# Expert stage 1 with 32 slots per expert in four 32-column tiles and 16 KB weight runs

## The reference

```python
D_MODEL = 1024; SEQ = 256; N_EXPERTS = 32; TOP_K = 2; EXPERT_FF = 512

def hier_moe(h, router_group_w, router_expert_w, w_gate, w_up, w_down):
    group_idx = argmax(h @ router_group_w)                 # 1 of 4 groups
    ...                                                    # top 2 of its 8 experts
    for each token n, each of its two experts e:
        a = h[n] @ w_gate[e]                               # 1024 -> 512
        b = h[n] @ w_up[e]
        out[n] += gate[n, e] * ((silu(a) * b) @ w_down[e]) # 512 -> 1024
```

## Time and profile before

| what | value |
|---|---|
| median of 3 runs | 2531.36 us (2530.78 to 2533.36) |
| span of the profiled execution | 2530.7 us |
| TensorE busy | 2299.3 us, 91% |
| VectorE busy | 1427.9 us, 56% |
| ScalarE busy | 1156.0 us, 46% |
| bytes moved | 653.96 MB, mean 258 GB/s |
| stage 1 in the span | about 258 to 779 us |

### The profile page before, as it was taken

The page is one execution under the profiler, slowest core; times in us unless marked ns, Lnnn a source line. Parts: engine busy times, 40 slices in busy tenths (PEclk is TensorE's granted clock), DMA queues, the critical chain, the costliest instruction groups (busy, mean ns, idle before and its releaser), DMA issues.

```text
span 2530.7 us, 31448 instructions
## 1 busy us (share of the span) xinstructions
PE 2299.3 (91%) x12724; PEld 1833.1 (72%) x12724; DVE 1427.9 (56%) x1373; ACT 1156.0 (46%) x999; POOL 289.0 (11%) x118
## 2 busy tenths in 40 slices
PE   6888899999997978998976789999999999999998
PEld 6877544444445977998875678787878787878786
DVE  4653211111113823453765178788888888888887
ACT  3521111111114523343543167676766766666765
POOL 4610000000002810002763000000000000000000
PEclk8998999999998999999988899999999999999999
DMA  7231699999995412555322159898989898989992
GB/s 258 91 128 67 238 394 394 394 394 394 394 394 183 138 51 84 185 183 183 134 100 100 67 199 366 306 365 308 368 305 370 302 370 308 365 312 361 335 335 112
DMA packets 286465, 653.96 MB, mean 258 GB/s; under 512 B 5312, under 2 KB 27968, under 8 KB 286144
## 3 DMA queue, kind: packets, MB, share of 16 engines
q1 hardware_dynamic: 286400, 653.01, 70.9%
HBM read 651.94 MB, written 1.05 MB: 258 GB/s over the span
## 4 chain that ended last, share of the span: by engine, by line
PE 78%; ACT 6%; DVE 6%; DMA 5%; issue 3%; POOL 1%; SPq 1%; ACTq 0%; POOLq 0%; DVEq 0%
PE psum L452 17%; PE psum L454 16%; PE psum L453 16%; PE psum L1395 7%; DMA ring<-in_w_up 5%; PE psum L582 3%; PE psum L1440 3%; PE psum L1380 2%; PE psum L1909 2%; PE psum L1422 2%; ACT arena_r L1737 1%; PE psum L1602 1%; DVE hT L435 1%; PE psum L425 1%; SPq L291 1%
## 5 line engine op out<-in xcount | busy, mean ns | idle before, releaser
L1796 DVE TENSOR_TENSOR ring_r<-ring,arena_r 128x2048 fp32r<-128x2048 f32 x338 | 766.6, 2288 | 175.8 <-ACT arena_r L1737 175.1
L1737 ACT ACTIVATE arena_r<-ring 128x2048 fp32r<-128x2048 f32 x338 | 633.3, 1911 | 221.6 <-PE psum L454 221.6
L453 PE MATMUL psum<-ring_r,arena_r 128*128 128x512 f32 (+1 forms) x1696 | 627.8, 370 | 0.0
L452 PE MATMUL psum<-arena_r 128*128 128x512 f32 (+1 forms) x1520 | 583.4, 384 | 15.2 <-DVE xT L1839 6.9
L454 PE MATMUL psum<-arena_r 128*128 128x512 f32 x1344 | 532.9, 397 | 0.0
L453 PEld LDWEIGHTS psum<-ring_r,arena_r 128*128 128x128 f32 x1696 | 320.8, 189 | 59.4
L452 PEld LDWEIGHTS psum<-arena_r 128*128 128x128 f32 x1520 | 286.2, 188 | 73.2 <-issue 11.8
L501 POOL TENSOR_TENSOR ring_r<-ring,ring_r 128x1024 fp32r<-128x1024 f32 x88 | 224.3, 2566 | 999.7 <-ACT ring_r L491 984.4
L454 PE MATMUL psum<-ring_r 128*128 128x256 f32 x1056 | 303.4, 287 | 0.0
L454 PEld LDWEIGHTS psum<-arena_r 128*128 128x128 f32 x1344 | 252.1, 188 | 59.2
L1395 PE MATMUL psum<-ring,arena 128*64 128x512 f32 x1024 | 224.5, 593 | 2.8 <-DMA ring<-in_w_up 1.8
(11 more groups left out here) (340 smaller groups left out, 2535.3 us busy)
## 6 DMA issues: line engine op xcount, KB each, us to landing
ring<-in_moe_w_gate SPq DMA_DIRECT2D x57, 2048.0 KB, 7.8
ring<-in_moe_w_up SPq DMA_DIRECT2D x56, 2048.0 KB, 7.8
ring<-in_moe_w_down SPq DMA_DIRECT2D x56, 2048.0 KB, 7.9
ring<-in_w_gate SPq DMA_DIRECT2D x32, 2048.0 KB, 15.7
ring<-in_w_down SPq DMA_DIRECT2D x32, 2048.0 KB, 12.6
ring<-in_w_up SPq DMA_DIRECT2D x32, 2048.0 KB, 19.3
ring<-in_c_w_in SPq DMA_DIRECT2D x8, 2048.0 KB, 9.1
ring<-in_w_in SPq DMA_DIRECT2D x7, 2048.0 KB, 17.5
```

The costliest lines, as they stand in the source:

```text
L452: nc.tensor.matmul(out, ah, bh, start=start, stop=False, **kw)
L453: nc.tensor.matmul(out, ah, bl, start=False, stop=False, **kw)
L1737: nc.scalar.activation(hi_buffer(j)[1], ring[:, m_ % SLOTS, half * HALF:(half + 1) * HALF], ACT.Copy).then_inc(weights_hi, 1)
L1796: nc.vector.tensor_tensor(ring_r[m_ % SLOTS][:, at], ring[:, m_ % SLOTS, at], hi_buffer(j)[1].bitcast(F32), ALU.subtract).then_inc(weights ...
```

## The change

C1 becomes 32, so two experts have 64 slots together (`PC`). Gate and up of both experts are now one group of matmuls: for each chunk k four tiles of 32 columns, gate 0, gate 1, up 0, up 1, which write partitions 0, 32, 64 and 96 onwards of bank 0. The down products also take four tiles, two experts by two halves of the result, in bank 2. Gathered tokens fit one bank and are copied in one step; the result is copied in two (L1530, L1531 of the changed file), from partitions 0 to 63 and 64 to 127. `gate_done` is gone: SP sends the gate and the up pieces when `up_done` arrives.

The rows of a weight piece are dealt as "(p k)": partition p gets eight (or four) neighbouring rows, one run of 16 KB. So that the products stay the same, the tokens' numbers are put in the matching order when they are transposed in the routing step, and the hidden values when silu is taken.

A trip starts with `share_transposed` and `spread_back` of the trip before, then gate/up, gather, down. The routing step writes its tables for eight rounds instead of four, with fewer and larger VectorE instructions.

```diff
-        C1, C2 = 64, 128
+        C1, C2 = 32, 128
         PASSES1, PASSES2 = T // C1, T // C2
...
-                return w[bass.ds(expert, 1), :, :].rearrange("e (k p) n -> p (e k) n", p=P), k, n
+                return w[bass.ds(expert, 1), :, :].rearrange("e (p k) n -> p (e k) n", p=P), k, n
...
-                    sp.wait_ge(moe_sems["moe1"][("gate_done", "up_done", "down_done")[s // 2]], i + 1)
+                    sp.wait_ge(moe_sems["moe1"]["up_done" if s < 4 else "down_done"], i + 1)
                     send(moe1_piece(expert[s % 2], s), s, landed["moe1"][s])
...
-                    sp.wait_ge(moe_sems["moe1"][("gate_done", "up_done", "down_done")[slot // 2]], trips1 + 1)
+                    sp.wait_ge(moe_sems["moe1"]["up_done" if slot < 4 else "down_done"], trips1 + 1)
...
-                    nc.scalar.activation(r_hrow[:, t * D + half * 512:t * D + half * 512 + 512], bank(2 * t + half),
-                                         ACT.Copy).then_inc(*s.step())
+                    row = r_hrow[:, t * D:(t + 1) * D]
+                    if m.groups:
+                        nc.scalar.activation(row.rearrange("p (k b c) -> p k b c", k=KC, b=KC)[:, :, 4 * half:4 * half + 4, :],
+                                             bank(2 * t + half).rearrange("p (b c k) -> p k b c", b=4, k=KC),
+                                             ACT.Copy).then_inc(*s.step())
+                    else:
+                        nc.scalar.activation(row[:, half * 512:half * 512 + 512], bank(2 * t + half),
+                                             ACT.Copy).then_inc(*s.step())
...
-            for p in range(m.passes):
-                do(nc.vector.tensor_copy(m.gate[:, :, m.per + p * n:m.per + (p + 1) * n], gt))
+            every = [P, NT, m.passes, n]
+            do(nc.vector.tensor_copy(m.by_pass(m.gate), gt.unsqueeze(2).to_broadcast(every)))
...
-            for p in range(1, m.passes):
-                do(nc.vector.tensor_scalar(w[:, 535 + p:536 + p], w[:, 534:535], float(p * m.slots), None, ALU.is_gt))
-            do(nc.vector.reduce_sum(w[:, 540:541], w[:, 536:535 + m.passes], AX_X))
+            over = w[:, 560:560 + m.passes - 1]
+            do(nc.vector.scalar_tensor_tensor(over, numbers[:, 1:], float(m.slots),
+                                              w[:, 534:535].to_broadcast([P, m.passes - 1]), ALU.mult, ALU.is_lt))
+            do(nc.vector.reduce_sum(w[:, 540:541], over, AX_X))
...
+        PC = 2 * C1
+        q_Xg, q_hidT = x_Xg[:, 0:KC * PC], x_hidT[:, 0:4 * PC]
+        q_silu, q_hid, q_y, q_shareT = (a[0:PC, :] for a in (x_silu, x_hid, x_y, x_shareT))
+
+        def pick_block(a, t, x, stride=PC):
+
+            return a[:, t * stride + x * C1:t * stride + (x + 1) * C1]
...
-                for r in range(2):
-                    for k in range(4 * r, 4 * r + 4):
-                        for t in range(NT):
-                            mm = nc.tensor.matmul(bank(7 - r)[:, (k % 4) * P:(k % 4 + 1) * P],
-                                                  r_hrow[:, t * D + k * P:t * D + (k + 1) * P],
-                                                  x_pick[:, t * P:(t + 1) * P], start=(t == 0), stop=(t == NT - 1))
-                    mm.then_inc(sem_["gathered"], 1)
+                pe.wait_ge(sem_["gathered_kept"], i + 1)
+                for k in range(KC):
+                    for t in range(NT):
+                        mm = nc.tensor.matmul(bank(7)[:, k * PC:(k + 1) * PC],
+                                              r_hrow[:, t * D + k * P:t * D + (k + 1) * P],
+                                              x_pick[:, t * PC:(t + 1) * PC], start=(t == 0), stop=(t == NT - 1))
+                mm.then_inc(sem_["gathered"], 1)
 
             def weights(i, what, x):
...
+
+                pe.wait_ge(sem_["gathered_kept"], i + 2)
+                pe.wait_ge(sem_["hidden_done"], i + 1)
+                w = [(weights(i, what, x).rearrange("p (k n) -> p k n", n=512), x) for what in "gu" for x in range(per)]
                 for k in range(KC):
-                    for x in range(per):
-                        mm = nc.tensor.matmul(bank(bank_)[x * C:(x + 1) * C, :],
-                                              x_Xg[:, k * P + x * C:k * P + (x + 1) * C], w[x][:, k, :],
+                    for n, (wx, x) in enumerate(w):
+                        mm = nc.tensor.matmul(bank(0)[n * C:(n + 1) * C, :],
+                                              q_Xg[:, k * PC + x * C:k * PC + (x + 1) * C], wx[:, k, :],
                                               start=(k == 0), stop=(k == KC - 1))
-                mm.then_inc(sem_["gate_done" if what == "g" else "up_done"], 1)
-
-            def gate_up(i):
-                pe.wait_ge(sem_["gathered_kept"], i * 2 + 3)
-
-                pe.wait_ge(sem_["silu_done"], i + 1)
-                gate_or_up(i, "g", 0)
-                pe.wait_ge(sem_["hidden_done"], i + 1)
-                gate_or_up(i, "u", 1)
-
-            def spread_back(i):
-
+                mm.then_inc(sem_["up_done"], 1)
+
+            def share_transposed(i):
                 pe.wait_ge(sem_["share_ready"], i + 2)
+
                 pe.wait_ge(sem_["spread_added"], i * 4 + 1)
                 for t in range(NT):
                     mm = nc.tensor.transpose(bank(4)[:, t * P:(t + 1) * P], x_share[:, t * P:(t + 1) * P], eye)
                 mm.then_inc(sem_["shareT_done"], 1)
+
+            def spread_back(i):
+
                 pe.wait_ge(sem_["y_kept"], i + 1)
                 pe.wait_ge(sem_["shareT_kept"], i + 2)
...
-                        mm = nc.tensor.matmul(bank(5 - r % 2)[:, j * T:(j + 1) * T], x_y[:, k * P:(k + 1) * P],
-                                              x_shareT, start=True, stop=True)
+                        mm = nc.tensor.matmul(bank(5 - r % 2)[:, j * T:(j + 1) * T], q_y[:, k * P:(k + 1) * P],
+                                              q_shareT, start=True, stop=True)
...
                 for f in range(4):
                     for half in range(2):
                         for x in range(per):
-                            mm = nc.tensor.matmul(bank(2 + half)[x * C:(x + 1) * C, :],
-                                                  x_hidT[:, f * P + x * C:f * P + (x + 1) * C],
+                            at = half * PC + x * C
+                            mm = nc.tensor.matmul(bank(2)[at:at + C, :], q_hidT[:, f * PC + x * C:f * PC + (x + 1) * C],
                                                   w[x][:, f, half * 512:(half + 1) * 512],
                                                   start=(f == 0), stop=(f == 3))
                 mm.then_inc(sem_["down_done"], 1)
...
             with pe.Fori(0, n) as i:
+                share_transposed(i)
+                spread_back(i)
                 gate_up(i)
-                spread_back(i)
-
-                pe.wait_ge(sem_["hiddenT_kept"], i + 1)
                 gather(i + 1)
                 down(i)
+            share_transposed(n)
             spread_back(n)
             return n
...
             def silu(i):
-                act.wait_ge(sem_["gate_done"], i + 2)
+                act.wait_ge(sem_["up_done"], i + 2)
 
                 act.wait_ge(sem_["hidden_done"], i + 1)
-                nc.scalar.activation(x_silu, bank(0), ACT.Silu).then_inc(sem_["silu_done"], 1)
+                nc.scalar.activation(q_silu.rearrange("p (f c) -> p f c", f=4),
+                                     bank(0)[0:PC, :].rearrange("p (c f) -> p f c", f=4), ACT.Silu)\
+                    .then_inc(sem_["silu_done"], 1)
...
-                nc.scalar.activation(x_shareT, bank(4)[:, 0:T], ACT.Copy).then_inc(sem_["shareT_kept"], 1)
+                nc.scalar.activation(q_shareT, bank(4)[0:PC, 0:T], ACT.Copy).then_inc(sem_["shareT_kept"], 1)
...
-                nc.scalar.activation(x_hidT, bank(6), ACT.Copy).then_inc(sem_["hiddenT_kept"], 1)
+                nc.scalar.activation(q_hidT.rearrange("p (f c) -> p f c", f=4),
+                                     bank(6).rearrange("p (f c) -> p f c", f=4)[:, :, 0:PC], ACT.Copy)\
+                    .then_inc(sem_["hiddenT_kept"], 1)
...
             with act.Fori(0, n) as i:
+                keep_share(i)
                 silu(i)
-                keep_share(i)
+                keep_hidden(i)
                 keep_gathered(i + 1)
-                keep_hidden(i)
 
                 act.wait_ge(sem_["down_done"], i + 2)
                 act.wait_ge(sem_["spread_done"], i * 4 + 5)
-                nc.scalar.activation(x_y, bank(2, 2), ACT.Copy).then_inc(sem_["y_kept"], 1)
+                nc.scalar.activation(q_y[:, 0:512], bank(2)[0:PC, :], ACT.Copy)
+                nc.scalar.activation(q_y[:, 512:1024], bank(2)[PC:2 * PC, :], ACT.Copy).then_inc(sem_["y_kept"], 1)
...
-                dve.wait_ge(sem_["up_done"], i + 2)
 
                 dve.wait_ge(sem_["hiddenT_done"], i + 1)
-                nc.vector.tensor_tensor(x_hid, x_silu, bank(1), ALU.mult).then_inc(sem_["hidden_done"], 1)
```

(43 more changed lines are left out.)

26 lines of the change are left out of this document (12 added, 14 removed).

## The result

The changed kernel takes 2544.59 us, the median of 4 runs (2543.3 to 2546.32), beside 2532.36 us for the kernel before, timed with it (4 runs, 2530.78 to 2535.51). The ratio is 1.0047, 95% interval 1.0034 to 1.0059: slower by 12 us, where 7 us faster was forecast. The profiled execution has a span of 2543.6 us against 2530.7, so the trace carries the whole difference.

A forecast was written before the change was run, and what follows sets the result against it. Weight transfer and TensorE were taken as level, about 31.5 us per trip. New trip: 0.1 + 4 x 4.90 + 2.6 + 9.3 = 31.6 us; 15 trips and ends change the time by -7.5, to 2524 us; range 2490 to 2560.

The forecast's parts named there:

- T: Length of one trip of expert stage 1: four transfers, latency and gate/up in series, forecast 31.6 us.
- ends: Stage's head and tail: first gate/up ends at about 282 (279 to 285), 15.0 us follow the last one.
- T = 32.1: Trip length in stage 1 at which the change would neither gain nor lose time.
- the latency: Weight wait of each trip: issue to first byte plus last byte to semaphore, 2.6 us (2.4 to 3.0).
- all that it called as before: Everything outside stage 1, claimed unchanged; next stage's first weights asked for early enough, so no cost.
- G = 9.3: Gate/up time per trip on TensorE: 6.9 us with four tiles overlapping plus 2.4 us for the slow clock.
- (b): Rival: clock stays low all through gate/up, trip 36.0 us, +58.5, 2590 us; chance 0.07.
- (c): Rival: four gate/up tiles overlap less than two do; partly 2558 us, chance 0.07; wholly 2626 us, chance 0.06.
- (d): Rival: long weight runs bring nothing (387 GB/s), trip 33.7 us, +24, 2555 us; chance 0.08.
- Rival (a): Clock in gate/up not lost or back at once; trip at DMA floor, 29.4 us, -40.5, 2491 us; chance 0.13.

The follow-up runs named there:

- the halves: Changed kernel with each gate and up piece loaded as two transfers, first halves asked for in the middle of gate/up, second at its end: 2499.48 us.
- the fill: Changed kernel with ten idle matmuls per trip, three ahead of the spread and seven ahead of gate/up: 2514.4 us, ratio to before 0.9922.
- asking late: Kernel before with the next gate pieces asked for when the up products are done, like the up pieces: 2563.27 us, ratio 1.0127.

## Why the forecast was wrong

The time lies inside the range of 2490 to 2560, 1.6 us above the forecast's own 2506 to 2543, and on the other side of no change. The forecast's model held: change = 15 T + ends. Its balance, T = 32.1, was 0.5 us above the forecast T, and three undersized terms (the latency, the ends and all that it called as before) crossed it together.

- **Right: the trip's form.** 16 trips, bounded by four transfers plus gate/up, down and hand-overs hidden. The chain of waits shows it. TensorE was to wait some 7 us in each trip and waits 5.2 (77.4/15), since the spread took longer; under the transfer that costs nothing.
- **Right: G = 9.3.** Four tiles overlap fully: 64 instructions in 7.07 us with the clock held, 7.07/64 = 110 ns each (forecast 107). The measured G was 9.3 in the mean, exact by some luck: 0.2 more for the tiles and 0.2 less for the clock cancel. It was 8.7 in the trip that starts at 437.50, where the clock rose 3.3 us after the restart, and 9.8 in the one before it. Rivals (b) and (c) fell. The Trainium skill (TensorE: Matmul & The Clock Gate, section "Measured speedup vs the span model") gives 3.07x for four row tiles. These four column tiles did better: four against two measured 13.73/7.07 = 1.94x, where 3.07 for four would leave 1.54.
- **Right: the rate.** 428 GB/s was taken; loaded windows show 401 to 459 GB/s, the halves reach six pieces at 4.87 us. Rival (d) fell: undoing the rows costs 27 us, where the rival's T said 31.
- **Right: what the clock costs in gate/up.** It is 9.3 - 7.1 = 2.2 us per trip, 33 us in all, close to the forecast (2.4). Without it the change would have been faster, as the fill shows, but it is no part of the miss. Rival (a) was the case with the clock held: its T of 29.4 came as 30.1 with the fill, since the wait is longer than I had it.
- **Wrong, the step that failed: the latency term, 2.6 us.** The trip's wait is 23.06 us, not 22.3. With four transfers of 4.90 and the 0.1 of issue, 3.3 to 3.4 us are left, outside the bounds of 2.4 to 3.0. Half of the miss was a choice: the one lone piece of this stage gave 8.4 - 5.4 = 3.0, and I went below it, towards the median of stage 2. In the changed kernel a lone piece of 16 KB runs gives 7.9 - 4.9 = 3.0 again. The other half is what a queue of four adds to that. Of the 3.4 us, 0.5 is the time without a byte (issue at 414.50, nothing before 415), and 1.2 is the slow start: 246, 180 and 328 GB/s in the three microseconds that follow, 0.75 MB where 428 GB/s would move 1.28. Some 1.6 are left, and the bytes come close to accounting for them: from 414.50 to 437.36 the engines moved 22.86 us x 396 GB/s = 9.05 MB, 0.66 more than four pieces, which is 1.5 us at 428 GB/s. They belong to the down pieces, asked for at 422.71. Whether they held up the last up piece or passed while its landing was being signalled is not shown. 0.76 us x 15 = 11.4 us, over half of the error. The Trainium skill (DMA: Bandwidth & Descriptors, section "Anatomy of one DMA") gives, for transfers issued from GpSimd, a fixed part of some 2.0 us beside the bytes at 436 GB/s. These are issued from SP; by those figures the wait would be an estimated 21.3 us. The trace shows 23.06, and agrees on the bytes' part alone (4.8 by that section, 4.9 here).
- **Wrong: the ends.** The head ended at 284.8 (forecast 282, top of its bounds 285) because gather, spread and the first half of gate/up ran at the low clock: 7.1, 7.2 and 9.5 us. The tail took 16.7 instead of 15.0: the clock fell 1.6 us into the last spread, behind short waits in the hand-over (0.56 and 1.51 us), so that spread took 5.66 and not 3.9. I had costed the clock behind the long wait only. In the stage's middle the slower spread is free, since it lies under the transfer; in head and tail nothing hides it. Together 4.5 us.
- **Wrong: "all else is as before".** The positions (0.8), the normalisation's matmuls on the low clock (0.8) and the later low stretches (3.0) add some 4.5 us. The first could have been read: a DMA that waits for the stage's end now follows the next stage's first piece by 16.6 us, where 31.2 us lay between them (747.35 to 778.56). The others can't be read from a trace of before.

In sum: 11.4 + 4.5 = 15.9 us in the stage, +8.4 instead of -7.5, and 4.5 behind it: 12.9 in place of -7.5. Not shown by any run here: why the restart's rate starts low, why the low stretches behind the stage fall where they do, and why asking late costs the kernel before more than the rate of the earlier trace rows accounts for.

## What to carry to other kernels

When an engine is sped up against a transfer that is level with it, look first at when the buffers are freed: four buffers freed at one moment put a full queue restart and the engine's own work in series, and asking for them in halves was worth 45 us, where the change as made lost 12. For the price of a restart take a lone piece of the same stage less its transfer (3.0 us here), not less, and leave room above it (3.4 here). Where the balance of a forecast lies within its terms' errors (0.5 us of a trip, 15 times), every term it calls nothing, the ends and the queue behind the stage among them, has to be costed.

## What the runs showed of the hardware

- Idle matmuls in a wait can pay where TensorE's work lies in series with a transfer: 30 us of 2544 for ten per trip, 23 for two. Seven per trip were worth nothing that can be told where the transfer alone sets the trip (2497.7 against 2499.5 us).
- The granted clock falls behind much shorter waits than the ones of 4.4 to 5.6 us in the earlier trace rows: with 2.80 us ahead of the spread it was 0.77 in the window 426 to 428, then 0.50. The length of the last wait doesn't settle it. With 1.46 and 1.61 us ahead of gate/up it stayed at 1.00; with 1.51 us ahead of the last spread it fell in the changed kernel (5.66 us) and not with the halves, where the same spread took 3.87 us.
- Two up pieces of 2 MB, asked for right behind two gate pieces, take SP 9.3 us to issue in 2 KB runs, and 1.2 us in 16 KB runs.
